# The y products move into the next interval's masked products, and the lora products between the halves of those

## The reference

```python
def rwkv7_group(p, mu, w0, w_up, a0, a_up, k_k, k_a, r_k, lnx_gain, lnx_bias):
    p = token_shift_lerp(p, mu)
    ...
    w_log = -jax.nn.softplus(-(w0 + jnp.tanh(wd) @ w_up)) - 0.5
    a = jax.nn.sigmoid(a0 + ad @ a_up)
    ...
    y = rwkv7_scan(rh, decay.reshape(B, T, H, N), kh, vh, kk, a.reshape(B, T, H, N))
    mean = jnp.mean(y, axis=-1, keepdims=True)
    var = jnp.mean(jnp.square(y - mean), axis=-1, keepdims=True)
    y = ((y - mean) * lax.rsqrt(var + LNX_EPS)).reshape(B, T, RWKV_WIDTH) * lnx_gain + lnx_bias
    ...
    return y * jax.nn.silu(g)
```

## Time and profile before

| what | value |
|---|---|
| median of 3 runs | 1840.0 us (1839.93 to 1843.25) |
| the profiled execution, its own time | 1838.4 us |
| its span, first to last instruction | 1836.5 us |
| busy: PE, PEld, DVE, ACT, POOL | 98%, 81%, 68%, 44%, 26% |
| granted TensorE clock, mean | 0.996 |

### The profile page before, as it was taken

The page is one execution under the profiler, slowest core; times in us unless marked ns, Lnnn a source line. Parts: engine busy times, 40 slices in busy tenths (PEclk is TensorE's granted clock), DMA queues, the critical chain, the costliest instruction groups (busy, mean ns, idle before and its releaser), DMA issues.

```text
span 1836.5 us, 37316 instructions
## 1 busy us (share of the span) xinstructions
PE 1806.4 (98%) x14530; PEld 1482.5 (81%) x14530; DVE 1240.2 (68%) x2240; ACT 814.6 (44%) x1682; POOL 481.6 (26%) x1096
## 2 busy tenths in 40 slices
PE   8999999999999999999999999999999999999996
PEld 6878888888888887888888888888888888888885
DVE  5876777776767777567777767777778764356433
ACT  7544435353535355444453535353544543242221
POOL 0014233241505060232332515060605051111110
PEclk9999999999999999999999999999999999999998
DMA  8633333333333335332333333333334543465443
GB/s 299 196 97 90 89 93 91 94 95 94 91 90 92 92 93 171 114 95 86 95 88 95 97 90 92 89 97 89 106 90 116 167 113 114 124 210 179 154 120 126
DMA packets 197840, 211.84 MB, mean 115 GB/s; under 512 B 98592, under 2 KB 103840, under 8 KB 197152
## 3 DMA queue, kind: packets, MB, share of 16 engines
q1 hardware_dynamic: 196800, 208.73, 39.6%
q10 hardware_dynamic: 864, 0.73, 0.1%
HBM read 187.37 MB, written 22.02 MB: 114 GB/s over the span
## 4 chain that ended last, share of the span: by engine, by line
PE 90%; DVE 3%; DMA 2%; POOL 1%; ACT 1%; issue 1%; SPq 0%; DVEq 0%; ACTq 0%; POOLq 0%
PE psum L1243 75%; PE psum L1228 3%; PE psum L1361 2%; PE psum L1301 2%; PE psum L1329 1%; PE psum L1511 1%; PE psum L1394 1%; PE psum L1475 1%; DMA work<-in_x_t 1%; PE psum L1482 1%; PE psum L1263 1%; POOL sub_t L534 1%; POOL sub_io L536 1%; PE psum L1464 1%; DVE w_lo L808 1%
## 5 line engine op out<-in xcount | busy, mean ns | idle before, releaser
L1243 PE MATMUL psum<-x_hi,w_hi 128*128 128x512 f32 x2144 | 864.5, 403 | 10.5 <-DVE x_lo L817 6.2
L1243 PE MATMUL psum<-x_hi,w_lo 128*128 128x512 f32 x2144 | 838.7, 391 | 0.0
L1243 PE MATMUL psum<-x_lo,w_hi 128*128 128x512 f32 x2144 | 838.2, 391 | 0.0
L808 DVE TENSOR_TENSOR w_lo<-w_raw,w_hi 128x512 fp32r<-128x512 f32 x536 | 376.2, 703 | 477.3 <-ACT w_hi L579 449.3
L579 ACT ACTIVATE w_hi<-w_raw 128x512 fp32r<-128x512 f32 x536 | 335.5, 629 | 734.0 <-PE psum L1243 639.2
L1243 PEld LDWEIGHTS psum<-x_hi,w_hi 128*128 128x128 f32 x2144 | 403.4, 188 | 105.9 <-DVE w_lo L808 10.1
L1243 PEld LDWEIGHTS psum<-x_hi,w_lo 128*128 128x128 f32 x2144 | 402.8, 188 | 87.5
L1243 PEld LDWEIGHTS psum<-x_lo,w_hi 128*128 128x128 f32 x2144 | 403.8, 188 | 76.8 <-issue 0.7
L534 POOL TENSOR_TENSOR sub_t<-sub_l,sub_io 128x60 f32<-128x60 f32 (+24 forms) x496 | 192.1, 387 | 850.5 <-DMA sub_l<-scratch_L 812.9
L536 POOL TENSOR_TENSOR sub_io<-sub_io,sub_t 128x60 f32<-128x60 f32 (+24 forms) x496 | 209.7, 423 | 38.9
L556 POOL TENSOR_TENSOR v<-v,kb 128x512 f32<-128x512 f32 x29 | 38.1, 1314 | 267.1 <-ACT kb L740 266.7
(11 more groups left out here) (249 smaller groups left out, 1833.7 us busy)
## 6 DMA issues: line engine op xcount, KB each, us to landing
w_raw<-in_w_in SPq DMA_DIRECT2D x408, 256.0 KB, 2.7
w_raw<-in_w_out SPq DMA_DIRECT2D x128, 256.0 KB, 2.7
sub_l<-scratch_L SPq DMA_DIRECT2D x16, 384.0 KB, 4.1
stage<-in_x_t SPq DMA_DIRECT2D x20, 256.0 KB, 4.4
stage<-scratch_MIX SPq DMA_DIRECT2D x19, 256.0 KB, 4.0
late<-in_x_t SPq DMA_DIRECT2D x16, 256.0 KB, 3.7
scratch_MIX<-sa SPq DMA_DIRECT2D x16, 256.0 KB, 3.5
scratch_MIX<-ym SPq DMA_DIRECT2D x16, 256.0 KB, 3.2
```

Source lines behind the costliest of these rows:

```text
L808: nc.vector.tensor_tensor(w_lo[gq % SPLIT][:], w_raw[gq % RAW][:], w_hi[gq % SPLIT][:].bitcast(F32), ALU.subtract).then_inc(w_ready, 1)
L1243: mm = nc.tensor.matmul(psum[:, bank_of(s)], wt[gq % SPLIT][:, cols], xx[:, c], start=(c == 0 and wt is w_hi and xx is x_hi), stop=(c == K ...
```

## The change

The y products get a function of their own, `outputs`. It stands in the next recurrence's quarter 1 (25 of its own), at the head, ahead of half 0 of the masked products; for i = 6 and 15, which have no recurrence right behind them, alone in quarter 25. The lora products stand between half 0 and half 1. DVE's reading of y (`read_y`) moves to quarter 25, ahead of the masks; `centre` to the end of quarter 25; ACT's square from 25 to 26, its root from 27 to 28; DVE's variance and norm from 26 and 27 to 27 and 28.

```diff
                     for j, at in current(gq):
+                        if j >= 1 and at == 25:
+                            read_y(j - 1)
+                    for j, at in current(gq):
                         if j >= 1 and at == 1:
                             masked(j - 1, 0)
                             masked(j - 1, 1)
...
                     for j, at in current(gq):
-                        if j >= 1 and at == 24:
+                        if j >= 1 and at == 25:
                             centre(j - 1)
...
-                    if at == 25:
+                    if at == 26:
                         act.wait_ge(y_centred, i + 1)
                         if i < INTERVALS - 1:
                             act.wait_ge(bonus_done, i + 2)
                         nc.scalar.activation(ysq[:], ym[:], ACT.Square).then_inc(y_squared, 1)
-                    if at == 27:
+                    if at == 28:
                         act.wait_ge(y_var, i + 1)
...
+                def read_y(i):
+                    dve.wait_ge(y_full, i + 1)
+                    dve.wait_ge(h_read, i + 1)
+                    for hh in range(2):
+                        ins = nc.vector.tensor_tensor(
+                            y[:, :, hh], psum[:, 4 + hh, 0:NB * HD].rearrange("p (b d) -> p b d", b=NB),
+                            hs[:, :, hh], ALU.add)
+                    then(ins)
+                    dve.sem_inc(y_read, 1)
...
+                def outputs(i):
+
+                    pe.wait_ge(gt_ready, i + 1)
+                    for b in range(NB):
+                        for c in range(2):
+                            for hh in range(2):
+                                rows = slice(hh * HD, (hh + 1) * HD)
+                                mm = nc.tensor.matmul(psum[vs_rows(c), 4 + hh, b * HD:(b + 1) * HD],
+                                                      gt[rows, b, c], states[rows, 2 * b + c],
+                                                      start=True, stop=True, skip_group_check=True)
+                    mm.then_inc(y_full, 1)
...
                 def recurrence(i, at):
                     if at == 1:
+                        if i not in (0, PAIRS - 1):
+                            outputs(i - 1)
                         products(i, 0)
+                        if i < INTERVALS - 1:
+                            lora_products(i + 1)
                         products(i, 1)
+                    if at == 25 and i in (PAIRS - 2, INTERVALS - 1):
+                        outputs(i)
```

More of the change, by code:

```diff
@@ L1112, in recurrence @@
                         transition(i)
[L1113 to L1122, removed]
+                    if at == 27:
                         dve.wait_ge(y_squared, i + 1)
@@ L1247, in quarter, with lora_products @@
                             mm.then_inc(w_used, 1)
-                def channels(j, at):
[L1250 to L1264, removed]
+                def lora_products(j):
+                    h = j // PAIRS
+                    pe.wait_ge(up_landed[j % 2], 16 * (j // 2 + 1))
+                    pe.wait_ge(lora_ready, 2 * h + 2)
+                    pe.wait_ge(rooted, h + 1)
+                    pe.wait_ge(inv_ready, j)
+                    pe.wait_ge(bonus_read, j)
+                    if j >= 2:
+                        pe.wait_ge(mixa_ready, j - 1)
+                    if j >= 3:
+                        pe.wait_ge(yt_read, PAIRS - 1 if j == PAIRS else j - 2)
+                    for x in range(2):
+                        rows = slice(x * LORA, (x + 1) * LORA)
+                        nc.tensor.matmul(psum[:, 2 + x], lora_up[j % 2][rows, :], lora[rows, :],
+                                         start=True, stop=True).then_inc(lora_done, 1)
+                def channels(j, at):
+                    if j == 0 and at == 3:
+                        lora_products(j)
                     if at == 4 and j % PAIRS == 0:
@@ L1487, in recurrence @@
                         chain(i, 2 * (at - 21) + 1)
[L1488 to L1497, removed]
                     if at == 31:
```

## The result

The changed kernel takes 1857.86 us, the median of 4 runs (1856.47 to 1858.87); the kernel before took 1840.16 us beside it (4 runs, 1839.93 to 1843.25). The ratio is 1.0097, 95% interval 1.0084 to 1.0110: slower by 1.0%. The forecast was 1857.0.

What follows compares the result with a forecast made beforehand. TensorE (PE), busy 98% of the span, was taken to bound the kernel. 13 x (1.35 - 0.15) = 15.6, 2.3 at i = 15 and 0.1 made 18.0 us on 1838.4: 1856.4; 1857 was forecast, range 1850 to 1864.

Steps and rivals of the forecast that it cites:

- Part 1: PE, quarter 24: without the y products, last chain product to first dense product takes 0.69 us, 0.77 us shorter.
- Part 2: PE, quarter 25: the y block makes it 0.62 us longer, lora order set to 0; net saving 0.15 us an interval.
- Part 3: PE's second half of products waits for y_read: fits by 0.2 us, except at i = 15, 2.3 us later once.
- Part 4: PE's transposes wait for sigma_w because late centre delays ACT's square and the sigmoids: 1.35 us, 13 times.
- Part 5: ACT and DVE: 13 more table loads of 1.28 us, effect on softmax's norm set to 0, upper end 0.48 us.
- A: Rival: the chain through ACT stays hidden, needing y_centred 1.35 us earlier; about 1836.4 us, or 1838.7; 6%.
- B: Rival: the products wait for y_read in every interval, mostly taken out of the transposes' stall; 1857 to 1860 us; 15%.
- C: Rival: the extra table load makes the softmax's norm late, 6.2 us more, 1863; 12%; or 24 us more, 1881; 2%.
- D: Rival: the square is late but less so, such as centre starting 0.4 us earlier; 5 us less, 1851; 10%.

Runs made afterwards that it cites:

- lora products last: Changed kernel with the lora products behind both halves of the masked products instead of between them: 1858.24 us, ratio 1.0101 to the kernel before.
- centre first: Changed kernel with DVE's centre right behind the reading of y, ahead of masks and shift; square still ahead of the sigmoids: 1852.27 us, ratio 1.0057.
- square behind: Changed kernel with ACT's square of y behind the three sigmoids of quarter 26 instead of ahead of them: 1844.09 us, ratio 1.0014 to the kernel before.
- norm-late kernel: Kernel before with only square, variance, root and norm one quarter later, PE's order and DVE's centre untouched: 1840.44 us, ratio 0.9998.
- y(14) back: Changed kernel with the y products of recurrence 14 and their reading kept in quarter 24 as before: 1852.99 us, ratio 1.0060 to the kernel before.
- SP's block moved: Changed kernel with square behind the sigmoids, y(14) in quarter 24, and additionally SP's block of quarter 12 one quarter later: 1840.13 us, ratio 1.0001.
- both cures, lora products last: Changed kernel with square behind the sigmoids, y(14) in quarter 24, and lora products behind both halves of the masked products: 1849.03 us, ratio 1.0048.

## Why the prediction was right, point by point

**Part 1 (saving of quarter 24).** 0.69 us forecast from L1527 to the first dense product, 0.70 measured.

**Part 2 (cost in quarter 25).** 3.46 forecast, 3.46 measured. The junction between the y products (64\*64) and the products (64\*128) was taken as dear as any other way out: 378.92 - 378.30 = 0.62 us in the changed kernel, just the 0.62 from y to bonus before. The Trainium skill, TensorEngine Tiling (Array Packing), Key Properties, says that a change of the tiling mode drains TensorE. The row agrees in so far as the way out costs the same into either mode; that it is a drain, no row shows. Lora in the middle costs nothing extra: 381.76 - 378.92 = 2.84, the same as in the old order.

**Part 3 (y_read).** The margin of 0.2 us held in the 13 intervals: read_y's row ends at 379.73 + 0.75 = 380.48, masks begin at 380.63, and the second half starts at 380.78, with no wait. "Without them PE would wait 0.7": 0.78 from start to start (0.51 of idle time) in the two kernels with the lora products last. The step that failed is a size: "PE is released ... 2.3 us later, once". The wait itself came as forecast: PE stood for 2.64 us where it had stood for 0.2 before. But it cost 4.8 us with what followed it. The two rows of the products at i = 15, and a window behind them (length, busy us of PE, PEld, DVE, ACT, POOL with counts, PEclk, DMA share, GB/s):

```profile
1465.73 1.16 PE L1309 MATMUL psum<-qr,kb 64*128 64x128 f32 x16
1469.53 2.08 PE L1309 MATMUL psum<-qr,kb 64*128 64x128 f32 x16 [2.64 <-DVEq L1095]
```

```profile
1470.00:1475.00 5.00, 5.00 (x24) 4.10 (x23) 3.90 (x7) 0.00 (x0) 0.00 (x0) 0.50 0.27 63
```

Sixteen products took 1.16 us ahead of the wait and 2.08 behind it, and the granted clock is 0.50, the lower level of 1.2 GHz, through the whole window and a little beyond (0.93 on average from 1475 to 1480). What that costs can be read against the kernel with centre first, where PE waited for 2.66 us at the same place and the clock stayed at 1.00. The transposes behind this quarter there, with the row of the wait, and then those of the changed kernel:

```profile
1464.44 1.16 PE L1307 MATMUL psum<-qr,kb 64*128 64x128 f32 x16 [2.66 <-DVEq L1095]
...
1471.11 1.03 PE L1230 MATMUL psum<-cst,kb 128*128 128x128 f32 x8
```

```profile
1479.07 1.03 PE L1232 MATMUL psum<-cst,kb 128*128 128x128 f32 x8
```

The same work took 1479.07 - 1469.53 = 9.54 us at the lower clock and 1471.11 - 1464.44 = 6.67 at the full one: 2.9 us more. The transposes gave 0.3 of this back (they start 0.23 us behind the last dense product now, and 0.54 before). The rest, 2.5 to 2.6 us, is the missing part: without it the place costs 0.62 for the y products, less 0.77 saved, and 2.64 - 0.19 more of waiting, 2.3 as forecast. The prediction's sum had no term for the clock.

**Part 4 (sigma_w).** Every step held: centre to square 386.84 - 385.12 = 1.72 (forecast 1.70), L632's end to PE's start 388.71 - 388.56 = 0.15 (0.14). The stall is 1.60 from the last dense product's start, against 0.24 where nothing waits (384.44 - 384.20 in the kernel with the square behind): 1.36, forecast 1.35. Centre began 385.12 - 378.92 = 6.20 us behind the first of the masked products, forecast 381.60 - 375.39 = 6.21. Setting the square behind the sigmoids takes all of the stall away (first experiment), and so does an early `centre` with PE's old order (the norm-late kernel).

**Part 5 (the rest of ACT and DVE).** The thirteen loads cost nothing that could be measured, by the kernel before with its norm late, but the margin was thinner than forecast: in the changed kernel PE's transposes behind the softmax start at 409.25, and DVE had gone on at 409.12, so 0.13 us of the 0.80 are left. The load began 0.02 us after the instruction ahead of it ended (403.39 + 0.63 = 404.02), and L660 began 405.33 - 404.04 = 1.29 us after the load did. The Trainium skill, ScalarE: Activation LUTs, What ACT_TABLE_LOAD costs, has a drain of 1380 ns beside the load; these rows show none. "Helps GpSimd's inverse and costs nothing" put a term at zero that was not: PE's wait at i = 6 became 2.3 us shorter, once. My reading, argued and not shown by a run of its own: the inverse, and behind it SP's block and the weight loads, start from masks that PE's stall doesn't delay, so they gain on a PE that is stalled behind them; SP's waits for the inverse fell from 52.4 us to 26.6 in all. PE's wait there was 0.5, 0.5 and 0.7 us in the three kernels with stalls at nearly every boundary (the changed one, y(14) back, lora last), 1.9 in the one with half the stall (centre first), and 3.1, 1.6, 2.0 and 2.5 in the four without. The kernel before had 2.8, but 0.7 with its norm one quarter later, so it is a wait that varies from one program to the next by 2 us. The 0.7 of the norm-late kernel, which has no stalls, speaks against my reading, and the cause stays open.

**The sum.** 18.0 forecast, 20.5 by the spans and 17.7 by the medians. It is partly luck that the median came within 1 us of the 1857 forecast: the clock at i = 15 (+2.5) and the relief at i = 6 (-2.3), neither of which stood in the sum, cancel. The 1.3 us of small steps have no cause that I can name, and the runs of the changed kernel alone differ by 2.4 us.

**The rivals.** A is out, since the thirteen stalls came; and the early y_centred that it asked for would not have been enough, as with centre first the stall was still 0.69 us. B's waits did not come; that they would be "taken out of the stall at the transposes" is what the lora products last showed. C is out by the norm-late kernel. D's 0.4 us less did not come.

## What to carry to other kernels

When an instruction moves a quarter later on an in-order engine, look at what stands behind it there and whether its input still comes in time: here a square that nobody hurried for held up two sigmoids that PE did need, and setting it behind them took away all 18 us of stalls. Waits in series on one engine need not add: an earlier one was free here as long as a later one was longer and the chain that released the later one did not pass through the earlier wait, and it cost its own length when the later one was cured. And price a wait of two or three microseconds on TensorE by the clock it may lose as well: at i = 15 it was as much again in the changed kernel, half of that with the square behind, and nothing with centre first.

## What the runs showed of the hardware

The clock behind a wait of PE is not decided by the wait's length alone. These are the waits of about two microseconds and more in the middle of the kernels, with the granted clock behind them:

| kernel | place | wait, us | clock behind it |
|---|---|---|---|
| changed | i = 15 | 2.64 | 0.50 from 1470 to 1475 |
| lora products last | i = 15 | 2.64 | 0.50 from 1470 to 1475 |
| square behind | i = 15 | 2.64 | 0.77 from 1455 to 1460, 0.89 from 1460 to 1465 |
| centre first | i = 15 | 2.66 | 1.00 |
| square behind | i = 6 | 3.07 | 0.50 from 694.4 to 700 |
| before | i = 6 | 2.81 | 1.00 |
| SP's block moved | i = 6 | 2.5 | 0.50 from 694.5 to 697 |
| both cures, lora products last | i = 6 | 2.0 | 0.77 from 699.3 to 706 |
| centre first | i = 6 | 1.9 | 1.00 |

The windows right behind the wait of 2.66 (centre first), of 2.81 (before) and of 3.07 (square behind):

```profile
1465.00:1470.00 5.00, 5.00 (x32) 4.11 (x29) 4.38 (x9) 1.15 (x2) 0.00 (x0) 1.00 0.13 47
```

```profile
693.70:700.00 6.30, 6.27 (x86) 5.03 (x87) 5.17 (x13) 3.08 (x7) 0.00 (x0) 1.00 0.65 221
```

```profile
694.40:700.00 5.60, 5.41 (x12) 3.81 (x12) 3.61 (x10) 0.00 (x0) 0.00 (x0) 0.50 0.71 233
```

The column ahead of the last two is the clock: 1.00, 1.00, 0.50. What decides it was not settled by these runs.
